# Modulation vectors from one multiply-and-sum per 128 features, instead of an accumulator that TensorE sums

## The reference

```python
mod = (jax.nn.silu(c) @ ada_w[layer] + ada_b[layer]).reshape(B, 3, 3, D)     # c is 1 x 1024, ada_w[layer] 1024 x 9216
h = modulate_pre(x, g[0, 0], mod[:, 0, 0], mod[:, 0, 1])                      # norm(x)*g*(1+scale) + shift
y = swiglu_ffn(h, ffn_w_in[layer, 0], ffn_w_out[layer, 0])
x = gated_post_add(x, y, g[0, 1], mod[:, 0, 2], 0.5)                          # x + 0.5*gate*norm(y)*g
...
mod = (jax.nn.silu(c) @ kv_ada_w + kv_ada_b)                                  # 2048 outputs, in the shared keys and values
...
mod = c_act @ w_ada[l] + b_ada[l]                                             # second block, c_act = silu(c_2), 1024 x 6144, l = 0, 1
```

## Time and profile before

| | us |
|---|---|
| median of 3 runs | 2412.24 |
| lowest, highest | 2407.43, 2412.79 |
| profiled execution: first to last instruction (span) | 2399.2 |
| what lies around the span (median less span; the execution profiled has no time of its own beside its span) | 13.0 |

### The profile page before, as it was taken

One profiled execution on the slowest core, in us unless ns is written; L12 is line 12 of the kernel. 1 busy time (PEld: TensorE's weight loads), 2 busy tenths in 40 slices (PEclk: granted clock), 3 DMA queues, 4 the chain that ended last, 5 costly groups with the idle time before them and its releaser, 6 DMA issues.

```text
span 2399.2 us, 43691 instructions
## 1 busy us (share of the span) xinstructions
PE 2315.6 (97%) x18388; PEld 2279.2 (95%) x18388; DVE 1532.9 (64%) x1387; ACT 973.9 (41%) x956; POOL 142.2 (6%) x210
## 2 busy tenths in 40 slices
PE   4999999999999999799999999999999999999998
PEld 4999999999899999589999999999999999999997
DVE  5877568775547765757776444758885435566554
ACT  2443444433423433544334444334443445334442
POOL 1000101110000000010001000001000000000000
PEclk7999999998879997899998999999998999999999
DMA  7988357994549953038964535448983544454552
GB/s 241 368 314 292 106 176 271 318 324 135 174 148 334 319 183 106 1 110 315 320 247 169 171 128 175 159 161 294 336 314 115 176 154 159 146 175 157 178 184 78
DMA packets 256366, 493.64 MB, mean 206 GB/s; under 512 B 16240, under 2 KB 145648, under 8 KB 255984
## 3 DMA queue, kind: packets, MB, share of 16 engines
q1 hardware_dynamic: 231920, 365.96, 45.8%
q0 software_dynamic: 24320, 125.84, 13.6%
HBM read 490.69 MB, written 1.05 MB: 205 GB/s over the span
## 4 chain that ended last, share of the span: by engine, by line
PE 92%; DVE 3%; ACT 2%; DMA 2%; issue 1%; SPq 0%; DVEq 0%; ACTq 0%
PE PA L502 14%; PE PA L504 14%; PE PA L503 14%; PE PY L502 7%; PE PY L504 7%; PE PY L503 7%; PE PB L502 5%; PE PB L503 5%; PE PB L504 5%; PE PB L556 2%; PE PB L545 2%; PE PA L563 2%; DMA adaw<-ada_w 1%; PE PY L836 1%; DVE rstd L1360 1%; ACT acc L1198 1%
## 5 line engine op out<-in xcount | busy, mean ns | idle before, releaser
L1312 DVE TENSOR_TENSOR wlo<-raw,whi 128x2048 fp32r<-128x2048 f32 x335 | 764.7, 2286 | 487.0 <-ACT whi L994 343.9
L502 PE MATMUL PA<-opA_hi,whi 128*128 128x256 f32 x2528 | 719.1, 284 | 1.3 <-DVE opA_lo L1371 1.3
L504 PE MATMUL PA<-opA_hi,wlo 128*128 128x256 f32 x2528 | 717.7, 284 | 0.0
L503 PE MATMUL PA<-opA_lo,whi 128*128 128x256 f32 x2528 | 717.7, 284 | 0.0
L994 ACT ACTIVATE whi<-raw 128x2048 fp32r<-128x2048 f32 x203 | 384.9, 1901 | 305.1 <-PE PA L504 140.0
L502 PEld LDWEIGHTS PA<-opA_hi,whi 128*128 128x128 f32 x2528 | 487.9, 193 | 1.9 <-issue 1.8
L503 PEld LDWEIGHTS PA<-opA_lo,whi 128*128 128x128 f32 x2528 | 487.8, 193 | 0.1
L504 PEld LDWEIGHTS PA<-opA_hi,wlo 128*128 128x128 f32 x2528 | 487.7, 193 | 0.0
L502 PE MATMUL PY<-opB_hi,whi 128*128 128x256 f32 x1344 | 386.1, 287 | 2.2 <-DVE opB_lo L1480 1.5
L503 PE MATMUL PY<-opB_lo,whi 128*128 128x256 f32 x1344 | 384.7, 286 | 0.0
L504 PE MATMUL PY<-opB_hi,wlo 128*128 128x256 f32 x1344 | 384.5, 286 | 0.0
(11 more groups left out here) (245 smaller groups left out, 2891.0 us busy)
## 6 DMA issues: line engine op xcount, KB each, us to landing
raw<-ffn_w_in SPq DMA_DIRECT2D x176, 512.0 KB, 5.2
raw<-w_in SPq DMA_DIRECT2D x144, 512.0 KB, 4.7
raw<-w_ff SPq DMA_DIRECT2D x128, 512.0 KB, 4.4
raw<-ffn_w_out SPq DMA_DIRECT2D x88, 512.0 KB, 4.7
adaw<-ada_w POOLq DMA_DIRECT2D x40, 768.0 KB, 6.3
mix<-ada_w POOLq DMA_DIRECT2D x32, 768.0 KB, 6.2
adaw<-w_ada POOLq DMA_DIRECT2D x32, 768.0 KB, 6.0
mix<-w_ada POOLq DMA_DIRECT2D x32, 768.0 KB, 6.1
```

The source lines that it names most:

```text
L502: nc.tensor.matmul(o_, w1, rhs(xh), start=start, stop=False, skip_group_check=True)
L503: nc.tensor.matmul(o_, w1, rhs(xl), start=False, stop=False, skip_group_check=True)
L504: return nc.tensor.matmul(o_, w2_, rhs(xh), start=False, stop=stop, skip_group_check=True)
L1312: TT(wlo[slot][:, 0:w], raw[slot][:, 0:w], whi[slot][:, 0:w].bitcast(F32), ALU.subtract).then_inc(lo_ready, 1)
```

## The change

The weights of the modulation are laid out output-major by the host (`adat`: 256 tiles of 128 outputs x 1024 inputs), so that an output has its own partition and its 1024 inputs lie along the row. silu(c) is then wanted as a row that is the same on all partitions: `crow`, 128 x 1024, loaded by a DMA that repeats one row of HBM, and put through SiLU by ACT (again with `c_2` ahead of `ffn11`). One DVE instruction multiplies a tile with `crow` and sums along the row into one column of `fresh` (L1276 of the new kernel; it appears as two instructions, the second writes the sum out). There are five slots of 128 x 1024 instead of four of 128 x 1536. The accumulator, its zeroing, `finish_mods` and `later` go; `mods` waits for DVE's own counter, and makes all scales and gates of a job at its end. Where `later` took the place of filler, filler stands again. SP's loads for the mixer move behind the first eight chunks of `mix0` and `mix1`, and the spatial weights go to `gact`.

```diff
@@ sync: loads of the first job, before = rows of 4 slots x 128x512, after = tiles of 128x1024
-            def first_ada(rows):
-                for k in rows:
-                    for slot, _, _, loads in JOBS["first"][1]:
-                        if k:
-                            sp.wait_ge(ada_used[slot], k)
-                        for w, c0, width, o in loads:
-                            sp.dma_start(slab[slot][:, o:o + width], w[k * P:k * P + P, c0:c0 + width]).then_inc(first_ready[slot], 16)
+            def first_ada(tiles):
+                for f in tiles:
+                    if f >= SLABS:
+                        sp.wait_ge(ada_used, f - SLABS + 1)
+                    sp.dma_start(slab[f % SLABS], I["adat"][f]).then_inc(first_ready[f % SLABS], 16)
...
                 if c0 == 0:
-                    first_ada(range(0, 6))
+                    first_ada(range(0, 13))
                 chunk(c0, src_ffn_in(w_in, 0, 0))
                 if c0 == 0:
-                    first_ada(range(6, KT))
+                    first_ada(range(13, 16))
                 chunk(c0 + 1, src_ffn_in(w_in, 0, 1))
...
+            sp.dma_start(crow[:], I["c_rows"][0:1].partition_broadcast(P)).then_inc(crow_in, 16)
             sp.dma_start(x[:], I["x_fm"]).then_inc(x_in, 16)
...
-                for slot in range(2):
-                    sp.wait_ge(ada_used[slot], ADA0["ff0"] + KT * l)
+                sp.wait_ge(ada_used, ADA0["ff0"][0] + 48 * l)
...
                 for g in range(12):
                     for h in range(2):
                         chunk(c + 2 * g + h, src_in512(I["w_in_2"][l], 512 * g, h))
+                    if g == 3:
+                        if l == 1:
+                            need(sp, "V", "b0.branch_done")
+                        sp.dma_start(wsr, I["ws"][l]).then_inc(lay_in, 16)
+                        sp.dma_start(bs, I["bs"][l:l + 1].partition_broadcast(P)).then_inc(lay_in, 16)
+                        sp.dma_start(wpool.rearrange("p (g k n) -> p g k n", g=4, k=2).rearrange("p g k n -> p (g k) n"),
+                                     I["w_pool"][l].rearrange("(g p) n -> p g n", p=P)).then_inc(lay_in, 16)
@@ tensor
-            def finish_mods(name):
-
-                n = LATER[name][0] if name in LATER else JOBS[name][2] // P
-                for slot in range(4):
-                    pe.wait_ge(ada_used[slot], ADA0[name] + KT)
-                take("B")
-                for t in range(n):
-                    last = nc.tensor.matmul(flat["B"][:, t:t + 1], acc[:, t * P:t * P + P], one, start=True, stop=True)
-                S(last, f"{name}.mods")
-                by("B", "V", f"{name}.mod")
...
                 outp(9, 9, False, False)
-                finish_mods(name)
                 outp(10, 10, False, True, c0 + 32, tag)
...
-                if l == 0:
-                    finish_mods("ff0")
                 outp(15, 15, False, True, c0 + 31, tag)
...
-                    idle(GAP_Y - (later(job_, 0) if job_ else 0))
+                    idle(GAP_Y)
...
-            for k in range(6, KT):
-                pe.wait_ge(ada_used[3], k)
-                idle(10)
-            finish_mods("first")
+            for f in range(9, 16):
+                pe.wait_ge(ada_used, f)
+                idle(6)
+            need(pe, "V", "first.mod")
             idle(14)
@@ vector
-            def ada(name, f, i=0, per=0):
...
-                STT(acc[:, o_:o_ + width], slab[slot][:, 0:width], cs, acc[:, o_:o_ + width],
-                    ALU.mult, ALU.add).then_inc(ada_used[slot], 1)
...
+            def ada(name, f):
+
+                g = ADA0[name][0] + f
+                if g < 16:
+                    dve.wait_ge(first_ready[g % SLABS], 16 * (g // SLABS + 1))
+                else:
+                    dve.wait_ge(ada_ready[g % SLABS], 16 * ((g - 16) // SLABS + 1))
+                nc.vector.tensor_tensor_reduce(slab[g % SLABS], slab[g % SLABS], crow[:], 1.0, 0.0, ALU.mult, ALU.add,
+                                               accum_out=fresh[:, f:f + 1]).then_inc(ada_used, 1)
+
+            def mods(name):
+
+                dve.wait_ge(ada_used, ADA0[name][0] + ADA0[name][1])
                 for t0, n, m0, bias in MODS[name]:
...
+                for j in range(1, 9):
+                    made(j)
+                    prep_to(c0 + 3 * j + 4)
+                    some(2)
+                    low(j)
+                    prep_to(c0 + 3 * j + 5)
+                    some(2)
+                    prep_to(c0 + 3 * j + 6)
+                    some(1)
@@ gpsimd
             def ada_all(name):
-                with pool.Fori(0, KT) as i:
-                    ada(name, i)
+                for g in range(ADA0[name][0], ADA0[name][0] + ADA0[name][1]):
+                    pool.wait_ge(ada_used, g - SLABS + 1)
+                    pool.dma_start(slab[g % SLABS], I["adat"][g]).then_inc(ada_ready[g % SLABS], 16)
...
+            pool.wait_ge(ada_used, ADA0["ffn11"][0])
+            pool.dma_start(crow[:], I["c_rows"][1:2].partition_broadcast(P)).then_inc(crow_again, 16)
             ada_all("ffn11")
```

More of the change, by code:

```diff
@@ L320, in G_ @@
             return gat[:, SUB[s]["i"] * 8:SUB[s]["i"] * 8 + 8]
-        ADA0, LOADS0, _n = {}, {}, 0
-        _loads = [0] * 4
-        for name, (_, slots, _) in JOBS.items():
-            ADA0[name] = _n
-            LOADS0[name] = list(_loads)
-            _n += KT
-            for q in range(4):
-                _loads[q] += KT * len(slots[q][3]) if name != "first" else 0
         def wv(w):
@@ L563, in idle @@
                     nc.tensor.matmul(flat["A"][:, 0:P], ident, onesD, start=True, stop=True)
-            def later(name, half):
-                n0, n1 = LATER[name][0], JOBS[name][2] // P
-                mid = (n0 + n1) // 2
-                for t in range(n0, mid) if half == 0 else range(mid, n1):
-                    last = nc.tensor.matmul(flat["B"][:, 512 + t:513 + t], acc[:, t * P:t * P + P], one, start=True, stop=True)
-                if half:
-                    S(last, f"{name}.mods2")
-                    by("B", "V", f"{name}.mod2")
-                return (mid - n0 if half == 0 else n1 - mid)
             def lo_of(tag):
@@ L684, in _ @@
             by("Y", "V", "00.u7")
-            boundary("00", "01", "ffn00")
+            boundary("00", "01")
             for g in range(6):
@@ L696, in _ @@
             by("Y", "V", "02.u7")
-            boundary("02", "10", "ffn01")
+            boundary("02", "10")
             for g in range(3):
@@ L752, in _ @@
             by("Y", "V", "10.u7")
-            boundary("10", "11", "ffn10")
+            boundary("10", "11")
             for g in range(2):
@@ L845, in _ @@
             by("Y", "V", "12.u7")
-            boundary("12", "b00", "ffn11")
+            boundary("12", "b00")
             for l in range(2):
@@ L1131, in _ @@
             act.wait_ge(vec_in, 16)
-            S(AC(csil[:], V("c", 0, 16), ACT.Silu), "csil")
+            act.wait_ge(crow_in, 16)
+            S(AC(crow[:], crow[:], ACT.Silu), "csil0")
             act.wait_ge(x_in, 16)
@@ L1215, in _ @@
             boundary("11", "12", CH["ffn11"], CH["ffn11"])
+            act.wait_ge(crow_again, 16)
+            S(AC(crow[:], crow[:], ACT.Silu), "csil1")
             ffn("ffn11")
@@ L1513, in ff2 @@
                 if l == 0:
+                    assert not todo
                     mods("ff0")
-            need(dve, "S", "csil")
-            need(dve, "G", "first.zero")
-            for k in range(KT):
-                if k == 5:
+            need(dve, "S", "csil0")
+            for f in range(16):
+                if f == 9:
                     inverse("00.x")
-                if k == KT - 1:
+                if f == 13:
                     prep_to(1)
-                for q in range(4):
-                    ada("first", 4 * k + q)
+                ada("first", f)
             mods("first")
@@ L1527, in _ @@
             ffn("ffn00")
-            boundary("00", "01", CH["conv_in"], CH["conv_in"], job_="ffn00")
+            boundary("00", "01", CH["conv_in"], CH["conv_in"])
             need(dve, "G", "cpad")
@@ L1556, in _ @@
             ffn("ffn01")
[L1557 removed]
+            boundary("02", "10", CH["kv"], CH["kv"], [("kv", "B"), ("10", "A")])
             prep_to(CH["cmp"] + 2)
@@ L1585, in _ @@
             ffn("ffn10")
-            boundary("10", "11", CH["nsa_in"], CH["nsa_in"], job_="ffn10")
+            boundary("10", "11", CH["nsa_in"], CH["nsa_in"])
             prep_to(CH["nsa_in"] + 8)
@@ L1658, in _ @@
             boundary("11", "12", CH["ffn11"], CH["ffn11"])
+            need(dve, "S", "csil1")
             ffn("ffn11")
-            boundary("12", "b00", CH["mix0"], CH["mix0"], job_="ffn11")
+            boundary("12", "b00", CH["mix0"], CH["mix0"])
             for l in range(2):
@@ L1847, in _ @@
             add_x("00")
-            need(pool, "T", "ffn00.mods2")
-            zero("ffn01")
             add_x("01")
```

204 lines of the change are left out of this document (64 added, 140 removed).

## The result

The changed kernel takes 2333.79 us (median of 4 runs, 2332.39 to 2336.95) against 2409.84 us for the kernel before (median of 4, 2407.31 to 2412.79): a ratio of 0.970, 95% interval 0.968 to 0.973. The span shrank from 2399.2 to 2330.9 us, by 68.3; the forecast took 61 from it.

The account below looks back on a forecast made before the run. TensorE, busy 97% of the span, was taken as the bound. Gains of 50.6 (column sums) and 12 (start), less 1.5 (DMA), make 61 us: span 2338, plus 13.0 to the median, 2351 us; range 2337 to 2368.

Parts of the forecast that it names:

- Part 1, windows: Ends of five feed-forwards: without column sums each window takes 7.52 us, gaining 55.4 us, less 2.8 for late pair sums.
- The control at the end of `ff1`: The same stretch without column sums, 7.52 us at clock 1.00, taken as the price of each changed window.
- The late chunk of `ffn11`: Chunk for `mix0` landing late in the `ffn11` window: costs 1.6 us of idle, counted in that window's 8.4 us gain.
- Part 1, filler instead of `later`: Where `later` did 12 column sums, filler of 128 columns costs about 0.25 us more each time, 2 us in all.
- Part 2: Start: more bytes under way and no column sums bring the first stage forward, 12 us gained, bounds 5 to 17.
- Part 3: New DVE instruction: about 1.35 us a tile, hidden in the feed-forward steps, cost 0; bunched loads in `ff0` cost 1.5 us.
- 13.0 us separate it from the median, and they stay: Whole time: the gap between the profiled span of 2399.2 us and the median of 2412.24 was added to the forecast span.
- A: Start not faster, from slow slot round trips or filler running on at the lower clock: 2358 us, chance 0.10.
- C: DVE just over the edge in `ff0` and its tail, a tile taking 1.6 us: 2363 us, chance 0.08.
- D: At five feed-forward ends another wait takes the column sums' place, 10 us less gain: 2361 us, chance 0.08.
- B: Feed-forward steps: a tile takes two passes, 2.35 us, DVE becomes the bound, 26 us slower: 2438 us, chance 0.06.
- 6.6 us of slack per feed-forward: Feed-forward steps: the chunk ring absorbs about 6.6 us of DVE lateness once, as splits end before they are wanted.

Follow-up runs that it names:

- the two runs with dead matmuls: Changed kernel with 160 matmuls that nobody reads put back where the column sums stood: 2378.53 us with one column each, 2358.39 us with 128.
- the ones: Changed kernel with 80 filler matmuls of 128 columns replaced by one-column matmuls at the places of the old `later`: 2340.02 us, ratio 0.9745.

## Why the prediction was right, and where its sizes were off

- *What bounds the kernel* was right: DVE's 256 new instructions cost nothing, and the time fell by what left TensorE's queue and the start.
- *Part 1, windows*: forecast 55.4 - 2.8 = 52.6, measured 52.6, or 52.0 with like ends; that it fits to the decimal is luck. The control at the end of `ff1` was the right price, and the estimate of 0.7 us for late pair sums met 0.70, 0.91, 0.70 and 0.69. That the clock is part of the cost was read from low clocks in a busy window, and the two runs with dead matmuls show it. The late chunk of `ffn11` was costed at the 1.6 us that were visible. What it would have cost with its cover gone, 8.5 us, was not worked out; it did not come due only because the change also issues that chunk 12.6 us earlier. The forecast named both causes, the last tile and the mixer's loads, but said "one split earlier"; the trace has 11.0 us from the tile.
- *Part 1, filler instead of `later`*: forecast a cost of 2.0, measured none. The step counted the instruction times of the filler (0.117 us for 128 columns) as if TensorE decided there; it waits 0.45 us for DVE's `opA_lo` behind its filler in both kernels, and the boundaries took 15.39, 15.39, 15.40 and 16.68 us before and 15.35 after. Behind `ffn11` it is even a gain, 2.6 us up to L923, now L865, in `mix0`. How much of that is the filler and how much the late chunk that went is not shown; put back into the changed kernel, the ones cost some 3 us.
- *Part 2*: forecast 12, measured 12.0 in one profile and 15.0 in the other. But "only the column sums and their wait would go, 5 us" was no floor. With as few bytes under way as before the start is 3.5 us slower than before.
- *Part 3*: a tile starts every 1.145 us and not every 1.35; the write-out lies beside the next instruction on DVE, which ACT's row of 190 ns could not tell. No step waits, so this changed no time. For the load in `ff0` 1.5 us were taken: the stretch from L923, now L865, in `mix0` to the window of `ff0` is 393.18 us in both kernels, so it costs nothing.
- *Sum*: 52.6 + 12.0 and 3.7 in the other stretches, where 52.6 + 12 - 2.0 - 1.5 = 61 had been forecast.
- *"13.0 us separate it from the median, and they stay"*: wrong. Each run whose span is on record, of either kernel, has only 1.6 to 1.8 us around it (2332.65 against 2330.9). By that the profiled execution of the kernel before had taken about 2401 us and was simply one of its shorter ones; its medians in the three later sets are 2400.78 to 2403.57. Against those the gain is 65 us (2400.78 - 2335.97), against the median of its own set 76. This step is why the forecast lay 17 us high: 13.0 - 1.7 = 11.3 of them here, 68.3 - 61 = 7.3 in the sum, less 1.1 by which the median lies above the profiled run.
- *Rivals*: A, C and D did not occur. B, the tile of two passes, did not either, but its price was tested: the way it worked out the step length met it to 0.1 us, its 6.6 us of slack per feed-forward were absent, and the lower clock was not in it. At 2.35 us a tile DVE would have cost over 100 us, not 80: an estimate from the 128 us at 2.415.

## What to carry to other kernels

Price a group of tiny matmuls by the window around it, in which the clock falls and stays low for what follows, and not by the instructions; a matmul of 128 columns can be the cheaper filler. Where the engine waits for another behind its filler, the length of the filler costs nothing. When a stall goes, work out what every late transfer under it costs without its cover, and count slack only for the buffer that has it, not for the engine's queue. Take the forecast from a span and the median of the same runs only if the profiled run's own time is known; if it is not, the gap between them may be nothing but spread.

## What the runs showed of the hardware

- Around 24 one-column matmuls (48 instructions, 7.26 us) the granted clock was 0.76 over 14.25 us, and 256-column matmuls behind them started 0.21 us apart instead of 0.12, for about 3 us; 24 of 128 columns took 5.52 us and left the clock at 1.00.
- DVE's product-and-sum of 128x1024 fp32 with an accumulator takes 1.22 us, its write-out 0.08 us, hidden.
- Waits of up to 3.5 us, in nearly every step of 19.87 us, cost TensorE more than themselves: 92 us more of waiting came with 37 us more of busy time, of which some 30 by the granted clock (0.965 against 0.976).
- The granted clock in the same stretch of one kernel was 0.95 in one execution and 0.91 in another, and the stretch 370.5 and 379.5 us.
- One core's DMA moved 229 GB/s with two loads of 512 KB under way and 378 with five.
